# Latent attention: scores, maxima and exponentials three units ahead of the values; conditioning turned half by half with transpositions

## What is computed

```
def adaln(c, w, b):                       # six vectors of 1024 per stream
    return jnp.split(silu(c) @ w + b, 6)

def mla_attend(q, k_all, v_all):          # 4 heads, 96 channels for q.k, 64 for v
    for qi in blocks_of_128(q):
        s = einsum('bqhd,bkhd->bhqk', qi, k_all) * scale
        p = softmax(s, axis=-1)
        o = einsum('bhqk,bkhd->bqhd', p, v_all)
```

## Time and profile before

| what | value |
|---|---|
| median of three runs | 4088.65 us |
| the profiled execution's own time | 4084.88 us |
| its span | 4083.1 us |
| latent attention, layer 0 | from 149 to 356 us |
| latent attention, layer 1 | from 2283 to 2465 us |
| mean granted TensorE clock | 0.978 |

### The profile page before, as it was taken

One profiled execution on the slowest core, in us unless ns is written; L12 is line 12 of the kernel. 1 busy time (PEld: TensorE's weight loads), 2 busy tenths in 40 slices (PEclk: granted clock), 3 DMA queues, 4 the chain that ended last, 5 costly groups with the idle time before them and its releaser, 6 DMA issues.

```text
span 4083.1 us, 77352 instructions
## 1 busy us (share of the span) xinstructions
PE 3856.5 (94%) x33178; PEld 3235.4 (79%) x33178; DVE 1977.1 (48%) x3607; ACT 1123.4 (28%) x2464; POOL 945.8 (23%) x699
## 2 busy tenths in 40 slices
PE   6999999899899999999998999999899899999997
PEld 5668888688787888888886669877788778888886
DVE  3455566444456333333357464556444564333446
ACT  3444242333323111111114452252333321000111
POOL 1000100222103333233223001100322033444442
PEclk8999999899999999999999999999999899999999
DMA  4230000100000011101111120001000101111111
GB/s 178 105 145 32 22 22 22 61 3 3 23 32 31 32 41 41 40 32 41 41 40 73 64 103 22 22 12 70 3 3 3 43 21 56 48 51 42 50 52 52
DMA packets 30526, 180.92 MB, mean 44 GB/s; under 512 B 2592, under 2 KB 7968, under 8 KB 15136
## 3 DMA queue, kind: packets, MB, share of 16 engines
q1 hardware_dynamic: 28944, 173.66, 11.5%
q10 hardware_dynamic: 1296, 3.07, 0.2%
HBM read 168.32 MB, written 8.39 MB: 43 GB/s over the span
## 4 chain that ended last, share of the span: by engine, by line
PE 85%; DVE 8%; ACT 4%; issue 2%; DMA 1%; POOL 1%; POOLq 0%; DVEq 0%; SPq 0%; ACTq 0%
PE ps L1355 37%; PE ps L764 9%; PE ps L774 8%; PE ps L799 4%; PE ps L897 3%; PE ps L1219 3%; PE ps L1227 2%; PE ps L1230 2%; PE ps L939 2%; PE ps L982 1%; PE ps L1308 1%; PE ps L1185 1%; PE ps L1282 1%; PE ps L1004 1%; PE ps L808 1%
## 5 line engine op out<-in xcount | busy, mean ns | idle before, releaser
L1355 PE MATMUL ps<-Yn_parts,ring_parts 128*128 128x512 f32 (+1 forms) x3888 | 799.0, 367 | 2.4 <-DVE Yn_parts L2589 2.1
L1355 PEld LDWEIGHTS ps<-Yn_parts,ring_parts 128*128 128x128 f32 x3888 | 671.3, 189 | 126.7 <-DVE Yn_parts L2589 5.4
L1355 PE MATMUL ps<-temp_parts,ring_parts 128*128 128x512 f32 (+1 forms) x2560 | 726.3, 369 | 5.0 <-DVE Hn_parts L2530 3.6
L2864 POOL TENSOR_TENSOR ring_parts<-ring,consts 128x2048 fp32r<-128x2048 f32 x62 | 286.4, 4620 | 1185.8 <-DMA ring<-in_ff 1185.8
L1355 PEld LDWEIGHTS ps<-temp_parts,ring_parts 128*128 128x128 f32 x2560 | 464.9, 189 | 88.0 <-DVE Hn_parts L2530 4.1
L2477 DVE SCALAR_TENSOR_TENSOR Xn<-ps,mods,Xn 128x256 f32<-128x256 f32 (+1 forms) x364 | 251.7, 691 | 575.0 <-PE ps L1355 504.6
L764 PE MATMUL ps<-ring_parts,Xn_parts 128*128 128x256 f32 x2560 | 504.3, 292 | 24.1 <-DVE Hn_parts L2109 16.2
L1355 PE MATMUL ps<-Hn_parts,ring_parts 128*128 128x512 f32 (+1 forms) x1280 | 471.4, 368 | 0.0
L764 PEld LDWEIGHTS ps<-ring_parts,Xn_parts 128*128 128x128 f32 x2560 | 417.1, 195 | 27.2 <-issue 22.6
L1913 ACT ACTIVATE Yn<-ps 128x256 f32<-128x256 f32 (+1 forms) x160 | 88.6, 554 | 1237.6 <-PE ps L1355 1237.6
L2588 DVE TENSOR_TENSOR Yn<-Yn 128x256 f32<-128x256 f32 (+1 forms) x160 | 186.8, 1167 | 402.8 <-ACT Yn_parts L1915 402.8
(11 more groups left out here) (317 smaller groups left out, 5817.1 us busy)
## 6 DMA issues: line engine op xcount, KB each, us to landing
ring<-in_ff SPq DMA_DIRECT2D x64, 1024.0 KB, 4.7
ring<-in_ada SPq DMA_DIRECT2D x22, 2048.0 KB, 8.9
ring<-in_halves SPq DMA_DIRECT2D x28, 1024.0 KB, 4.7
Xn<-in_x SPq DMA_DIRECT2D x1, 5120.0 KB, 15.3
Hn<-in_ada SPq DMA_DIRECT2D x2, 2048.0 KB, 21.1
Xn<-in_x SPq DMA_DIRECT2D x2, 2048.0 KB, 18.2
kept_x<-Xn SPq DMA_DIRECT2D x4, 1024.0 KB, 4.6
Xn<-kept_x SPq DMA_DIRECT2D x1, 4096.0 KB, 15.0
```

What stands on the lines that cost most here:

```text
L1355: m = pe.matmul(ps[:, bank, 0:hi - lo], w[a][:, k, j * P:(j + 1) * P], x[b][:, k, lo:hi], start=(k == 0 and part == 0), stop=(k == k_n - 1 ...
L2864: link(TT(by(half_hi[s]), by(half[s]), spread(ones, 1, HALF // P), ALU.mult))
```

## The change

Scores, maxima and exponentials run three units ahead of the values instead of two. The turning of a conditioning vector is split into two halves, one for each chunk, each with four plain transpositions of 128x128; the second half comes one iteration after the first. The sum over the four groups moves to VectorE, as a reduction that reads 32 elements per row out of the bank, in front of the bias. The stream's waits follow: each chunk's buffer is free after its own half.

```
-                for step, what in enumerate((("rows", 2 * c), ("rows", 2 * c + 1), ("cond", c))):
-                    at_[5 * c + 2 + step if c else (-2, -1, 1)[step]] = what
+                for step, what in enumerate((("rows", 2 * c), ("rows", 2 * c + 1), ("cond", 2 * c), ("cond", 2 * c + 1))):
+                    at_[5 * c + 2 + step if c else (-2, -1, 1, 2)[step]] = what
...
             def ada_turn(bank):
-                pe.wait_ge(sems["ada_kept"], state["rows"])
-                for s_ in range(2):
-                    kept = chunk_at(state["chunk"] - 2 + s_)[:, 0:512]
-                    for j in range(4):
-                        m = pe.matmul(ps[:, bank, (s_ * 4 + j) * 2:(s_ * 4 + j) * 2 + 2], kept[:, j * P:(j + 1) * P], cst["pick"],
-                                      start=True, stop=True, skip_group_check=True)
+                s_ = state["ada"] % 2
+                pe.wait_ge(sems["ada_kept"], state["ada"] + 1)
+                kept = chunk_at(state["chunk"] - 2 + s_)[:, 0:512]
+                for j in range(4):
+                    m = turn(ps[:, bank, j * P:(j + 1) * P], kept[:, j * P:(j + 1) * P])
...
                 ada_turn(7)
+                ada_turn(6)
...
                 conditioning(-2)
                 conditioning(-1)
+                scores(2, 0)
+                scores(2, 1)
                 for n_ in range(n_units):
...
-                    if n_ + 2 < n_units:
-                        scores(n_ + 2, 0)
-                        scores(n_ + 2, 1)
+                    if n_ + 3 < n_units:
+                        scores(n_ + 3, 0)
+                        scores(n_ + 3, 1)
...
+                exps(2)
...
-                    if n_ + 2 < n_units:
-                        exps(n_ + 2)
+                    if n_ + 3 < n_units:
+                        exps(n_ + 3)
...
-                m = STT(out, ps[:, bank, 0:16].rearrange("p (a b) -> p a b", b=2), 0.5, spread(ada_b[:, L, 8 * v:8 * v + 8], 2, 2),
-                        ALU.mult, ALU.add)
+                at_ = slice(8 * v + 4 * half_, 8 * v + 4 * half_ + 4)
+                out = mods[:, L, at_, :]
+                link(dve.tensor_reduce(out, ps[:, bank, :].rearrange("p (a g x) -> p a x g", a=4, g=4)[:, :, 0:2, :], AX.X, ALU.add))
+                m = STT(out, out, 0.5, spread(ada_b[:, L, at_], 2, 2), ALU.mult, ALU.add)
...
                 divide(0)
+                rowmax(2)
...
-                    if n_ + 2 < n_units:
-                        rowmax(n_ + 2)
+                    if n_ + 3 < n_units:
+                        rowmax(n_ + 3)
```

More of the change, by code:

```diff
@@ L673, in load @@
                 if n_ in (4, 5):
-                    sp.wait_ge(sems["ada_mm"], 1)
+                    sp.wait_ge(sems["ada_mm"], n_ - 3)
                 i, signal = STREAM[:n_].count(STREAM[n_]), chunk_signal(n_)[0]
@@ L682, in load @@
                     if STREAM[held] == "ada":
-                        sp.wait_ge(sems["ada_mm"], (STREAM[:held + 1].count("ada") + 1) // 2)
+                        sp.wait_ge(sems["ada_mm"], STREAM[:held + 1].count("ada"))
                     else:
@@ L911, in bank_of @@
                         if kind == "cond":
-                            pe.wait_ge(sems["ada_sum"], rows_ahead(L) // 2 + n_ + 1)
+                            pe.wait_ge(sems["ada_sum"], rows_ahead(L) + n_ + 1)
                     return bank
@@ L2048, in flat, with ada @@
                 return ap.rearrange("p a b -> p (a b)")
-            def ada(L, v, bank=7):
+            def ada(L, v, half_, bank):
                 if state["ada"] == 0:
@@ L2058, in ada @@
                 dve.wait_ge(sems["ada_mm"], state["ada"])
-                out = mods[:, L, 8 * v:8 * v + 8, :]
-                m = STT(out, ps[:, bank, 0:16].rearrange("p (a b) -> p a b", b=2), 0.5, spread(ada_b[:, L, 8 * v:8 * v + 8], 2, 2),
-                        ALU.mult, ALU.add)
+                at_ = slice(8 * v + 4 * half_, 8 * v + 4 * half_ + 4)
+                out = mods[:, L, at_, :]
+                link(dve.tensor_reduce(out, ps[:, bank, :].rearrange("p (a g x) -> p a x g", a=4, g=4)[:, :, 0:2, :], AX.X, ALU.add))
+                m = STT(out, out, 0.5, spread(ada_b[:, L, at_], 2, 2), ALU.mult, ALU.add)
                 if v in (1, 4):
@@ L2235, in latent_attention @@
                         divide(n_ + 1)
-                    if n_ + 2 < n_units:
-                        rowmax(n_ + 2)
+                    if n_ + 3 < n_units:
+                        rowmax(n_ + 3)
                     if n_ in ada_at and ada_at[n_][0] == "cond":
-                        ada(*ADA_WITH[L][ada_at[n_][1]], users[ada_at[n_]][0])
+                        ada(*ADA_WITH[L][ada_at[n_][1] // 2], ada_at[n_][1] % 2, users[ada_at[n_]][0])
                 out(n_units - 1)
@@ L2693, in _ @@
                     ln.barrier()
-                    ada(0, 0)
-                    ada(0, 1)
+                    for v in range(2):
+                        for half_ in range(2):
+                            ada(0, v, half_, 7 - half_)
                     ln.barrier()
```

## The result

| | before | changed |
|---|---|---|
| median in the same comparison | 4084.81 us (20 runs, 4081.70 to 4092.48) | 4091.41 us (20 runs, 4084.63 to 4097.34) |
| the profiled execution's own time | 4084.88 us | 4090.36 us |
| its span | 4083.1 us | 4088.6 us |

The ratio is 1.0012, 95% interval 1.0006 to 1.0017: by it the changed kernel is about 4.9 us slower (2.5 to 7), inside the 0.2% that I had called no difference, and inside the range. The two medians lie 6.6 us apart, the two means 5.0.

What follows compares the result with a forecast made beforehand. TensorE, busy 94% of the span, was taken as the bound. Layer 0 +4.7, layer 1 -0.8 and the start -1.1 sum to +2.8 us, on 4087.2 for no change: 4090 us, eight-in-ten range 4083 to 4097.

Steps and rivals of the forecast that it cites:

- The pairs: Layer 0's alternating full and short units: wait moves before the full unit's third chunk, 2.04 us; pair 7.78 instead of 7.40.
- Full units, the tail: Full units stay at 4.64 us; at each layer's end the 1.13 us wait moves one unit earlier, about 0.4 per layer.
- The halves: Each half-turning on TensorE takes 0.46 us, VectorE's reduction 0.20, bank wait 0.1, or 0.3 where a further scaling follows.
- The reduction is dear: Rival: VectorE's reduction costs 0.60 us and more, bank wait grows 0.4 in 20 places, 4098 us; chance 0.06.
- The start: Conditioning before the attention: first half turned while the second is copied, VectorE's sum ready at 35.26; -1.1 us, at worst 0.
- Layer 0: Layer 0's attention: TensorE's waits 7.7 to 17.4 us, conditioning work 5.0 less; +4.7 us.
- Layer 1: Layer 1's attention: TensorE's waits 4.8 to 7.4 us, conditioning work 3.4 less; -0.8 us.
- One at a time: Whole kernel, each part walked by itself: the lead alone +5.8 us, the conditioning alone -4.3.
- Costed at nothing: Chunk loads, and VectorE's added work under 0.6 us per half, were taken to add no time except the bank wait.
- The lead does what it says: Rival: the alternating pairs' waits vanish, 12.8 us in iterations 0 to 12; -10 us, 4077 us; chance 0.06.
- Only the conditioning counts: Rival: alternating units cost no more than before, the lead's 5.8 falls away; -3 us, 4084 us; chance 0.18.
- The clock falls in the longer pauses: Rival: clock falls in units 0 to 15, pauses 2.0 us, price 1.7 each; all eight pairs 4104 us; chance 0.05.

Runs made afterwards that it cites:

- exps_late: Changed kernel with the long exponentials of layer 0's full units 4 to 14 one iteration later on ScalarE, behind the full unit's copies: 4082.51 us, ratio 0.9996 to before.
- sum_first: Changed kernel with VectorE doing a half's sum and bias before the row maximum of that iteration: 4094.42 us, ratio 1.0024 to the kernel before.
- lead_only: Kernel before with only the lead of three units, conditioning turned as before: 4092.85 us, ratio 1.0021 to the kernel before.
- after_padded: Changed kernel with 64 empty instructions (drain) at the head of TensorE's program: 4087.61 us, ratio 1.0006 to the kernel before.
- halves_only: Changed kernel with the lead put back to two units, conditioning still turned by halves: 4079.07 us, ratio 0.9987 to the kernel before.
- two_shorts_sum_first: Changed kernel with lead two, layer 0's short units ahead of the full ones, VectorE's sum before the row maximum: 4072.29 us, ratio 0.9969 to before.
- again 1: Second profile of the unchanged kernel before: 4088.72 us, layer 0's attention 211.3 us with four stretches at the low clock.

## Why the prediction was right, point by point

- **The pairs.** Right in place, cause and size: a wait of 2.04 us was forecast before the full unit's third chunk, about 1.95 was found, and the pair takes 7.78. `exps_late` shows the cause.
- **Full units, the tail.** As forecast: 4.64 us bare, the 1.12 us wait has moved to unit 37 (345.57) and unit 38 waits 0.34.
- **The halves.** 0.46 forecast, 0.44 found; the reduction 0.20 and 0.19; the bank wait with a further scaling 0.3 and 0.28, and all of layer 1's bank waits 1.8, by `sum_first` 1.8. "The reduction is dear" falls.
- **The start.** -1.1 forecast, -1.3 found: the last bias is ready at 34.88 + 0.17 us, where 35.26 stood in the working.
- **Layer 0.** +4.7 forecast, +4.2 found, each profile with one low stretch. Two terms were each too large and made up for each other: TensorE idle grew from 6.2 to 14.1, by 7.9 where I had 9.7, and its busy time fell by 3.7 where I had 5.0 (a span less a busy time in the windows above). That the sum comes within 0.5 is in part luck. The modelled ends of matmuls blur both; their difference is what the stage shows.
- **Layer 1.** -0.8 forecast and found, in the same way: idle +1.9 for 2.6, work -2.7 for 3.4.
- **One at a time.** +5.8 and -4.3 forecast, +8.6 and -5.3 measured, with intervals of some 3.7 us to each side. The profile of `lead_only` has three low stretches in its attention stages, that of the kernel before one.
- **"Costed at nothing".** Here the working failed. My terms give +2.8 and the profiles +2.1 for them; the measured difference is +4.9. I had taken the code outside the attention as unchanged in time. It isn't: the last output lands 2.4 us later. Another 0.7 in the stretch after layer 1's attention lies in unchanged code too (it stays in `after_padded`: 1619.1 against 1618.5), and its cause is open. The same stretch took 1615.9 to 1621.0 us in the single profiles of the seven other kernels, less 2.4 where the landing was late, so 0.7 is small beside what edits elsewhere went with.
- **The rivals.** "The lead does what it says" falls as the change stands; the time that it would give, 4077, is that of an order which the change doesn't have. "Only the conditioning counts" falls by the pairs and by `lead_only`. "The clock falls in the longer pauses" is right as to the mechanism and wrong as to the price. By the prediction's own sign the forecast would be wrong "if the granted clock falls in the pauses", and it did fall after them: once, three times and not at all in the three profiles of the changed kernel, four times in `sum_first`. But most of the pauses left it at 1.00, and the kernel before lost as much in another place, behind its turnings, which the prediction did not see: it had put its one low stretch into both kernels alike. The rule of the Trainium skill ("TensorE: Matmul & The Clock Gate", Part 4: PE-mode transpose), that transpositions don't count as busy for the clock gate in the same way, finds no support in these runs, in which they always stand among many other matmuls: `halves_only` and `two_shorts_sum_first` have all the added transpositions and a granted clock of 1.00 in layer 0's attention, and no low stretch of the ten followed a half without a pause of 1.78 us or more just before.

The forecast of 4090 us lay 1.4 below the measured median, and that it came so near is luck: the sum of +2.8 was 2 us too small by the ratio, 3.8 by the medians, and the 4087.2 taken for no change was 2.4 too high, since the kernel before had a median of 4088.65 in the first three runs and of 4084.81 beside the changed one.

## What to carry to other kernels

A longer lead moves every instruction of the leading step on every in-order queue, not only on the one that is to gain. With units of two sizes by turns, an odd shift puts the long step of one before the short step of the other: write down for each queue what now stands ahead of the piece that the busiest engine waits for. Against the changed kernel it helped to lead by different amounts on different engines, and more to group the units by size; but in both orders the lead of two came out ahead: 4079.07 against 4091.41 by turns, and grouped 4073.83 against 4077.55, where the intervals overlap and the stage's 1.5 us show it.

When two versions differ by a few microseconds, compare the stages in which no line changed before explaining the total.

## What was not expected of the hardware

- In the profiles with one packet of instructions (16 KB, 0.95 us) in the midst of the last output, a sixteenth of that output's last 512 KB followed behind it, and the landing came 2.4 us later in a 4.1 ms kernel. 64 empty instructions in an idle place took packet and delay away.
- The granted clock fell right behind a run of 16 matmul instructions of two columns, with TensorE busy all the time (0.57 over 278 to 282 us in the kernel before, again 1). Where transpositions did the same work, it fell only behind pauses of 1.78 us and more.
- The granted clock of one and the same stage varied from 0.97 to 0.99 in three executions of the kernel before and from 0.98 to 1.00 in three of the changed one; between executions of one kernel that was up to 4.9 us (213.9 against 209.0) in layer 0's attention, as much as the difference under study.
